# The last four rows of x in the two norms between stages of a decoder layer: computed by GpSimd instead of VectorE

## What is computed

```python
def rms_norm(x, g):
    y = x * lax.rsqrt(jnp.mean(x * x, axis=-1, keepdims=True) + EPS)
    return y * g

# mixers -> u (320 x 2048)
x = x + rms_norm(u @ w_out, g_post_mix)                  # norm 0, its first half
h = rms_norm(x, g_pre_x)                                 #         its second half
x = x + rms_norm(cross_attend(h, w_xq, mem_k, mem_v, w_xo), g_post_x)   # norm 1, first half
h = rms_norm(x, g_pre_ffn)                               #         second half
y = conv_ffn(h, ...)                                     # begins with h @ w_up
```

## Time and profile before

| what | value |
|---|---|
| runs shown | 2720.48, 2720.12, 2718.70 us |
| median | 2720.12 us |
| the profiled execution's own time | 2720.43 us |
| its span, first to last instruction | 2718.9 us |
| PE busy | 2677.2 us (98%) |
| DVE busy | 1604.5 us (59%) |
| ACT busy | 1064.8 us (39%) |
| GpSimd busy | 237.2 us (9%) |
| norm 0, from the first DVE product with the root to the start of tile 2 on PE | 1420.64 to 1444.20 us |
| norm 1, the same | 1762.06 to 1785.63 us |

### The profile page before, as it was taken

The page is one execution under the profiler, slowest core; times in us unless marked ns, Lnnn a source line. Parts: engine busy times, 40 slices in busy tenths (PEclk is TensorE's granted clock), DMA queues, the critical chain, the costliest instruction groups (busy, mean ns, idle before and its releaser), DMA issues.

```text
span 2718.9 us, 49344 instructions
## 1 busy us (share of the span) xinstructions
PE 2677.2 (98%) x20086; PEld 2553.9 (94%) x20086; DVE 1604.5 (59%) x2387; ACT 1064.8 (39%) x1339; POOL 237.2 (9%) x337
## 2 busy tenths in 40 slices
PE   8999999999999999999999999999999999999998
PEld 7999887899999999999989969999999999999998
DVE  5564564476777767777546334495655555563333
ACT  4333454444444444444334234343323223243233
POOL 0102311011111111111100000001100000010000
PEclk9999999999999999999999999999999999999999
DMA  9746656765555555555564694546655555555555
GB/s 259 215 127 153 219 174 205 233 195 150 154 151 157 156 150 157 149 158 157 133 201 125 215 391 121 145 125 172 160 154 148 145 154 146 143 142 151 149 148 162
DMA packets 694726, 458.72 MB, mean 169 GB/s; under 512 B 14268, under 2 KB 662044, under 8 KB 688492
## 3 DMA queue, kind: packets, MB, share of 16 engines
q1 hardware_dynamic: 680860, 413.32, 53.9%
q0 software_dynamic: 9936, 28.48, 4.0%
q10 hardware_dynamic: 3792, 14.88, 1.5%
HBM read 429.91 MB, written 26.72 MB: 168 GB/s over the span
## 4 chain that ended last, share of the span: by engine, by line
PE 93%; DVE 3%; DMA 2%; ACT 1%; issue 1%; POOL 0%; POOLq 0%; DVEq 0%; SPq 0%; ACTq 0%
PE psum L607 20%; PE psum L612 20%; PE psum L609 20%; PE psum L863 4%; PE psum L1297 4%; PE psum L1295 4%; PE psum L1296 4%; PE psum L868 2%; PE psum L1005 1%; PE psum L1008 1%; PE psum L1001 1%; PE psum L1176 1%; PE psum L721 1%; PE psum L1017 1%; DMA ring<-in_w_in 1%
## 5 line engine op out<-in xcount | busy, mean ns | idle before, releaser
L607 PE MATMUL psum<-x_high,w_high 128*128 128x320 f32 x3808 | 1123.9, 311 | 0.7 <-ACT w_high L2064 0.5
L609 PE MATMUL psum<-h_low,w_high 128*128 128x320 f32 x3312 | 974.3, 309 | 0.0
L1349 DVE TENSOR_TENSOR w_low<-ring,w_high 128x2048 fp32r<-128x2048 f32 x292 | 675.7, 2314 | 310.9 <-ACT w_high L2064 310.4
L2064 ACT ACTIVATE w_high<-ring 128x2048 fp32r<-128x2048 f32 x294 | 561.7, 1911 | 672.5 <-PE psum L612 545.6
L607 PEld LDWEIGHTS psum<-x_high,w_high 128*128 128x128 f32 x3808 | 713.2, 188 | 6.3 <-issue 2.4
L609 PEld LDWEIGHTS psum<-h_low,w_high 128*128 128x128 f32 x3312 | 622.0, 188 | 1.6
L612 PE MATMUL psum<-x_high,w_low 128*128 128x320 f32 x3808 | 597.4, 309 | 0.0
L612 PEld LDWEIGHTS psum<-x_high,w_low 128*128 128x128 f32 x3808 | 568.5, 188 | 0.0
L1295 PE MATMUL psum<-y_high,w_down_high 128*128 128x320 f32 x704 | 218.2, 310 | 1.2 <-DVE w_low L1968 1.2
L1297 PE MATMUL psum<-y_high,w_low 128*128 128x320 f32 x704 | 218.4, 310 | 0.0
L1296 PE MATMUL psum<-y_low,w_down_high 128*128 128x320 f32 x704 | 216.7, 308 | 0.0
(11 more groups left out here) (433 smaller groups left out, 2910.0 us busy)
## 6 DMA issues: line engine op xcount, KB each, us to landing
ring<-in_w_in SPq DMA_DIRECT2D x128, 1024.0 KB, 5.8
ring<-in_w_up SPq DMA_DIRECT2D x88, 1024.0 KB, 5.7
ring<-in_w_down SPq DMA_DIRECT2D x64, 704.0 KB, 4.8
ring<-in_w_xk SPq DMA_DIRECT2D x16, 1024.0 KB, 5.7
ring<-in_w_xv SPq DMA_DIRECT2D x16, 1024.0 KB, 5.1
ring<-in_w_out SPq DMA_DIRECT2D x16, 1024.0 KB, 6.1
ring<-in_w_xq SPq DMA_DIRECT2D x16, 1024.0 KB, 6.1
ring<-in_w_xo SPq DMA_DIRECT2D x16, 1024.0 KB, 6.1
```

What stands on the lines that cost most here:

```text
L607: mm(out, w_hi[:, j % 2, k, :], x_hi[:, k, :], start=k == 0, stop=False)
L609: mm(out, w_hi[:, j % 2, k, :], lo[:, k, :], start=False, stop=False)
L1349: V.tensor_tensor(w_lo[:, j], ring[:, j], w_hi[:, j % 2].bitcast(FP32), ALU.subtract).then_inc(N.slab_lo, 1)
L2064: F(w_hi[:, j % 2], ring[:, j], ACT.Copy).then_inc(N.slab_hi, 1)
```

## The change

In both norms `add(3)` leaves DVE. GpSimd makes the product of chunk 3 with the root (it starts when `add(0)` is done, which shows that `rstd` is there) and the addition to `xT`, in two instructions of 128 x 1280. `n_x` then counts three chunks a norm; ACT and DVE wait for chunk 3 on a semaphore of GpSimd's (`idx_zero`).

```diff
@@ between, on DVE
 def low_rows(q):
-    dve.wait_ge(N.n_x, 4 * i + q + 1)
+    if q < 3:
+        dve.wait_ge(N.n_x, 3 * i + q + 1)
+    else:
+        dve.wait_ge(N.idx_zero, 6 + i)
...
 low_rows(0)
 add(2)
 low_rows(1)
-add(3)
 low_rows(2)
 low_rows(3)
@@ between, on ACT
 for q in range(4):
-    act.wait_ge(N.n_x, 4 * i + q + 1)
+    if q < 3:
+        act.wait_ge(N.n_x, 3 * i + q + 1)
+    else:
+        act.wait_ge(N.idx_zero, 6 + i)
@@ GpSimd
 G.memset(qm, 0.0).then_inc(N.qm_zero, 1)
+
+def last_rows(i):
+    pool.wait_ge(N.n_x, 3 * i + 1)
+    h, x = hT[:, 12:16], xT[:, 12:16]
+    root = rstd.rearrange("p (o t) -> p o t", o=1).broadcast_to([P, 4, T])
+    G.tensor_tensor(h, h, root, ALU.mult).then_inc(N.qm_zero, 1)
+    pool.wait_ge(N.qm_zero, 2 + 2 * i)
+    G.tensor_tensor(x, x, h, ALU.add).then_inc(N.idx_zero, 1)
+
+last_rows(0)
 pool.wait_ge(N.slab_used, B_XQ + KD)
 G.memset(pxm, 0.0).then_inc(N.qm_zero, 1)
+last_rows(1)
 pool.wait_ge(N.conv_evac, 1)
```

More of the change, by code:

```diff
@@ L1870, in _ @@
             dve.wait_ge(N.px_T, 1)
-            dve.wait_ge(N.qm_zero, 2)
+            dve.wait_ge(N.qm_zero, 3)
             for b in range(DB):
@@ L1903, in x_rows_turned @@
             def x_rows_turned(q):
-                dve.wait_ge(N.n_x, 8)
+                dve.wait_ge(N.n_x, 6)
+                dve.wait_ge(N.idx_zero, 7)
                 V.transpose(x_turned.rearrange("p b k d -> p k b d")[:, 4 * q:4 * q + 4],
```

## The result

The changed kernel takes 2726.46 us (median of 7 runs), the kernel before, run beside it, 2718.86 us: 7.6 us more, a ratio of 1.0029 with a 95% interval of 1.0019 to 1.0038. The interval does not hold 1, so the changed kernel is slower, by 0.2 to 0.4%. Forecast were 7.0 us and 2727.1.

The account below looks back on a forecast made before the run. PE bounds the kernel (93% of the span), so its standing still in the norms counts. Each norm costs 2 x 2.68 of holds less 1.85 returned, 3.5 us; 2720.1 + 7.0 = 2727.1 us, range 2724.5 to 2731.

Parts of the forecast that it names:

- GpSimd holds DVE up, by turns: In both norms, GpSimd and DVE instructions reading SBUF alternate; DVE's order runs 5.36 us late after two turns.
- The size of a hold: Time one GpSimd instruction of 1280 columns holds DVE up in the norms: 2.68 us, bounds 2.14 and 2.86.
- What comes back: Of the 2.92 us taken off DVE per norm, only 1.85 returns, as ACT's squares and PE's products end last.
- Chunk by chunk: Norm 0: ACT takes chunk 2 at 1437.88, chunk 3 at 1440.9; PE pauses about 5 us; tile 2 at 1447.7.
- The covers: Behind chunk 2's addition, DVE's low rows are covered by 1.4 us; the third slab's low part does not end last.
- its 3.2 us: In norm 0 the third slab's low part comes some 3.2 us later, by 1450.3; PE needs it at 1452.4.
- The clock: PE, starting low again after its pause, finishes chunk 1 at about 1439.1, before chunk 2's last row; costs nothing.
- The rival: Clock rival: PE's 5 us pause costs over 4.4 us of slow work; 0.8 to 3.2 us a norm; chance 0.12.
- no holding up: DVE's float32 instructions in the norms run free of GpSimd; 1.8 us gained a norm, 2716.5 in all; chance 0.07.
- short holds: Both GpSimd instructions hold DVE 2.14 us; a norm costs 2.4 us, 4.9 in all, 2725.0; chance 0.09.
- DVE first: GpSimd gets its turn only in DVE's gap, chunk 3 ready at 1441.6; 4.4 us a norm, 2728.9; chance 0.06.

Follow-up runs that it names:

- e2: Kernel before, plus in norm 0 a same-size GpSimd pair on data nobody needs there; 4.0 us over the kernel before (1.0008 to 1.0026).
- e3: Kernel before, plus in norm 0 two GpSimd memsets of 128x2048, which only write; -0.8 us against the kernel before (0.9990 to 1.0008).
- e6: Changed kernel with GpSimd's two four-row instructions cut into eight of one row (128x320); 6.5 us over the kernel before (1.0017 to 1.0039).
- e4: Kernel before without root product and addition for x's last four rows, both norms, every engine; -3.5 us against the kernel before (0.9979 to 0.9997).
- e10: Changed kernel with 24 more unused PE products in its pause ahead of chunk 1; 7.7 us over the kernel before (1.0017 to 1.0037).
- e1: Changed kernel with the change in norm 0 only, norm 1 as before; 3.6 us over the kernel before (1.0005 to 1.0024).
- e8: Changed kernel with GpSimd taking two of the last four rows, DVE the other two; 3.3 us over the kernel before (1.0009 to 1.0027).
- e7: Kernel before, plus one unneeded 128x1280 GpSimd addition in norm 0 while DVE waits; -0.2 us against the kernel before (0.9993 to 1.0011).

## Why the prediction was right

- *GpSimd holds DVE up, by turns.* Shown, by the rows of the changed kernel, by e2 (without anybody who waits for the result) and by e3 (without reads). The order of turns, GpSimd ahead of DVE's next instruction each time, is that of the rows after and of e6's eight.
- *The size of a hold.* 2.68 us was taken, 2.73 and 2.56 came, 5.29 for the pair against 5.36. The bounds were 2.14 and 2.86. The estimate of 2.8 us from the Trainium skill (GPSIMD Engine Reference, section "Elementwise — side-by-side cycle accounting") was above both.
- *What comes back.* 1.85 us was worked out from chunk 3 following chunk 2 behind ACT's squares; 5.29 - 3.49 = 1.80 came back, and e4 shows the same 1.8 with no hold at all. That the sum was met to 0.01 us a norm is in part luck: the holds were taken 0.07 us too long and the gain 0.05 too large, and the two cancel.
- *Chunk by chunk.* ACT's chunk 2 was expected 17.2 us behind the first product with the root and chunk 3 20.3; they came at 17.19 and 20.18. PE's pause ahead of chunk 1 was to be about 5 us and was 5.33; tile 2 was to be at 27.1 and came at 27.06 and 27.05.
- *The covers held.* The last low rows were there before PE asked for them, and the third slab's low part too (1446.74 to 1449.03, asked for some 4.8 us into tile 2). DVE waited 0.54 us for ACT's squares ahead of the latter. The prediction doesn't name that wait, but its 3.2 us contain it.
- *The clock cost nothing in the changed kernel*, as forecast: PE was through chunk 1 at 18.4 us behind the first product, when it had chunk 2's first rows waiting but not the last, and it took chunk 3 as ACT brought it (the table of e10). But the margin is small, and that it held in both norms of the profiled execution is partly luck. In e1 and e6, with the clock low for 1.5 us longer or at another place, it cost 0.65 and 1.1 us in one norm, in e8 and e10 0.3 and 0.2. The rival had a chance of 0.12 and a price of 0.8 to 3.2 us a norm; what was seen lies at the lower end of that or below it.
- *The rest.* 0.6 us of the measured 7.6 is outside the norms or within what the runs scatter; nothing in the profile ties it to the change.

Fallen are the rival of no holding up, short holds, and DVE first. The time by itself, 7.6 us more with an interval of 5.2 to 10.3, excludes the first, barely the second (4.9) and not the third (8.8); the holds of 2.73 and 2.56 us and the order of the turns in the profile exclude both. What is not shown is the clock in the executions that were not profiled: e1 shows that it can cost 0.65 us in a norm with the same DVE rows.

## What to carry to other kernels

An idle engine is no free engine if it reads through what a busy one reads through: here GpSimd took 1.9 to 2.1 ns of VectorE's time for each column of an instruction on two different float32 tensors, and VectorE does the column itself in 1.2. Look for rows in which the two already meet, and for a VectorE instruction far over its usual duration beside a GpSimd one; the price can be read off before the change is made. GpSimd's work was free where VectorE was idle (e7), and where GpSimd only wrote (e3).

What is taken off the engine that sets the pace comes back only as far as the next one in the line: 1.8 of 2.9 us here, so the whole idea had a ceiling of 0.13%.

## What the runs showed that was not expected

- A GpSimd addition of a tile to itself held VectorE up for 2.00 us, an addition of two tiles of the same size 2.56 (2.65 in e10), a product with a broadcast row 2.73 (128x1280 each). In the kernel before, the 64x1024 product of rows 11 had 1.71 us. Holds go by more than the columns; by what was not tried. Part of the step from 2.73 to 2.56 comes with the VectorE instruction that is held and not with GpSimd's: in e6 the product of VectorE (L1809) lost 0.68 and 0.67 us and its addition (L1810) 0.56 both times, with GpSimd's products beside the first pair and its additions beside the second.
- The clock's low level is less regular than one execution shows. Behind pauses of 4.7 to 5.3 us PE worked at 0.50 for 3.5, 4.0, 4.5 and 5.5 us before it came back. And it fell to 0.51 in e10 after a pause of only 1.49 us, 1.4 us into the work, and in e6 behind pauses of 1.79 and 2.14 us, while pauses of 0.51 and 1.10 us in the kernel before left it at 1.00.
